# Rotary embedding: the exchange of rows inside SBUF by matrix product, or by sixteen-kilobyte transfers with the sign in the angle table

## What is computed

```python
def _partial_rope(t, cos, sin):
    tr = t[..., :ROT_DIM].astype(jnp.float32)            # ROT_DIM = 16
    t1, t2 = tr[..., :ROT_DIM // 2], tr[..., ROT_DIM // 2:]
    rot = jnp.concatenate([t1 * cos - t2 * sin, t2 * cos + t1 * sin], axis=-1)
    return jnp.concatenate([rot.astype(t.dtype), t[..., ROT_DIM:]], axis=-1)

q_a = _partial_rope(_rmsnorm_2(q_a.reshape(b, s, ATTN_HEADS, HEAD_DIM), g_qn_attn[l]), cos, sin)
k_a = _partial_rope(_rmsnorm_2(k_a.reshape(b, s, ATTN_HEADS, HEAD_DIM), g_kn_attn[l]), cos, sin)
```

## Time and profile before

| | us |
|---|---|
| median of 3 runs | 2988.92 (2987.07 to 2989.79) |
| span of the profiled execution | 2986.5 |
| PE busy with matrix products in it | 2817.0 (94%) |
| VectorE (DVE) busy | 1155.4 (39%) |
| ScalarE (ACT) busy | 556.1 (19%) |
| GpSimd (POOL) busy | 621.8 (21%) |

### The profile page before, as it was taken

How to read it: one execution, slowest core, us unless ns; L and a number is a source line. 1 busy time by engine, 2 the same in 40 slices (tenths; PEclk the granted TensorE clock), 3 DMA queues, 4 the chain that set the end, 5 groups by cost and what they waited for, 6 DMA issues and landing times.

```text
span 2986.5 us, 42182 instructions
## 1 busy us (share of the span) xinstructions
PE 2817.0 (94%) x18274; PEld 2423.2 (81%) x18274; DVE 1155.4 (39%) x2204; ACT 556.1 (19%) x856; POOL 621.8 (21%) x584
## 2 busy tenths in 40 slices
PE   8999999999999999999999999999999999866766
PEld 6888988889888899899988888889988888533433
DVE  3865235452433334745214344435355312210111
ACT  2101222124211101010033116210012330100000
POOL 0001411122121075068601210038800000000000
PEclk9999999999999999999999999999999999988878
DMA  9764543344443556764544444365433328899998
GB/s 406 297 263 163 175 150 134 121 141 171 140 141 127 196 199 229 272 219 166 183 147 143 139 153 143 130 224 170 165 135 130 105 91 351 381 432 430 430 430 371
DMA packets 74155, 641.62 MB, mean 215 GB/s; under 512 B 8304, under 2 KB 9584, under 8 KB 17648
## 3 DMA queue, kind: packets, MB, share of 16 engines
q1 hardware_dynamic: 71376, 631.55, 56.5%
q10 hardware_dynamic: 2592, 7.33, 0.6%
HBM read 637.80 MB, written 1.05 MB: 214 GB/s over the span
## 4 chain that ended last, share of the span: by engine, by line
PE 86%; DMA 12%; DVE 1%; issue 0%; ACT 0%; POOL 0%; SPq 0%; DVEq 0%; POOLq 0%; ACTq 0%
PE ps L1364 27%; PE ps L1340 20%; PE ps L1386 13%; DMA work<-in_w_moe 11%; PE ps L1561 7%; PE ps L1397 3%; PE ps L1591 2%; PE ps L1374 2%; PE ps L1145 2%; PE ps L1450 1%; PE ps L1167 1%; PE ps L1568 1%; PE ps L1272 1%; PE ps L1536 0%; PE ps L1539 0%; DMA ring<-in_w 0%
## 5 line engine op out<-in xcount | busy, mean ns | idle before, releaser
L2760 POOL TENSOR_TENSOR ring<-ring 128x512 f32<-128x512 f32 (+1 forms) x294 | 374.2, 1301 | 783.0 <-DMA ring<-in_w 315.7
L1364 PE MATMUL ps<-ring 128*128 128x256 f32 x2368 | 517.4, 380 | 0.6 <-ACT ring L1784 0.6
L1364 PEld LDWEIGHTS ps<-ring 128*128 128x128 f32 x2368 | 447.3, 190 | 63.2 <-issue 2.4
L2029 DVE TENSOR_TENSOR work<-work,ps 128x128 f32<-128x128 f32 (+3 forms) x534 | 185.6, 386 | 714.6 <-PE ps L1340 349.2
L1340 PE MATMUL ps<-work,ring 128*128 128x128 f32 x3312 | 385.8, 275 | 0.3 <-POOL work L2760 0.3
L1386 PE MATMUL ps<-work,ring 128*128 128x256 f32 x1760 | 385.5, 380 | 0.0
L1340 PEld LDWEIGHTS ps<-work,ring 128*128 128x128 f32 x3312 | 377.6, 192 | 0.5 <-POOL work L2760 0.5
L1386 PEld LDWEIGHTS ps<-work,ring 128*128 128x128 f32 x1760 | 332.5, 190 | 46.2 <-issue 2.1
L1364 PE MATMUL ps<-h,ring 128*128 128x256 f32 x1408 | 310.7, 382 | 6.5 <-ACT h L1784 2.9
L1364 PEld LDWEIGHTS ps<-h,ring 128*128 128x128 f32 x1408 | 265.8, 191 | 47.0 <-issue 5.7
L2029 DVE TENSOR_TENSOR work<-work 128x128 f32<-128x128 f32 (+4 forms) x566 | 261.6, 511 | 52.1 <-ACT eb L1812 24.9
(11 more groups left out here) (315 smaller groups left out, 2655.6 us busy)
## 6 DMA issues: line engine op xcount, KB each, us to landing
ring<-in_w SPq DMA_DIRECT2D x210, 1024.0 KB, 4.9
work<-in_w_moe SPq DMA_DIRECT2D x22, 4096.0 KB, 33.5
ring<-in_w_moe SPq DMA_DIRECT2D x22, 4096.0 KB, 33.4
ring<-in_w_in SPq DMA_DIRECT2D x80, 1024.0 KB, 4.9
work<-in_w_ada SPq DMA_DIRECT2D x40, 1024.0 KB, 6.1
ring<-in_w_ada SPq DMA_DIRECT2D x32, 1024.0 KB, 5.1
ring<-in_w SPq DMA_DIRECT2D x28, 768.0 KB, 4.2
ring<-in_w_out SPq DMA_DIRECT2D x16, 1024.0 KB, 5.1
```

The source lines that it names most:

```text
L1364: last = nc.tensor.matmul(ps[:, b, c * L:c * L + L], w[:, k * L + c * P:k * L + c * P + P], hs[cols][:, k, :], start=(k == 0), stop=(k == ...
L2029: return nc.vector.tensor_tensor(o, i0, i1, op)
L2760: return nc.gpsimd.tensor_tensor(o, i0, i1, ALU.subtract)
```

## The change

The product with `rot`, the matrix itself, its load and the semaphore `nq_rot` go. In the stage `rotate` ACT's queue now waits for `nq_done` (and, from the third on, for the DVE to be through with the rotation two before), and then issues four transfers inside SBUF, each of 8 partitions by 512 numbers (16 KB), which write the exchanged halves of the tile into `tmp2`. The DVE waits for all four, multiplies `tmp2` in place by the table of sines, and does the rest as before. `tmp2` is set to zero once, ahead of the DVE's first `nsum`, so that the rows that no transfer writes stay zero. The sign moves into the table: the frequencies of the first half are negated, which negates its sines and leaves the cosines.

```diff
@@ PE
-                    elif kind == "rotate":
-                        i = stage[1]
-                        pe.wait_ge(nq_done, i + 1)
-                        if i >= 2:
-                            pe.wait_ge(nq_roped, i - 1)
-                        nc.tensor.matmul(ps[:, 6 + i % 2, :], rot, normed(i), start=True, stop=True).then_inc(nq_rot, 1)
@@ ACT
-                        for dst, name in ((amask, "amask"), (blk64, "blk64"), (rot, "rot"), (rw[:], "rw"),
+                        for dst, name in ((amask, "amask"), (blk64, "blk64"), (rw[:], "rw"),
                                           (counting, "tri")):
...
+                    elif kind == "rotate":
+                        i = stage[1]
+                        act.wait_ge(nq_done, i + 1)
+                        if i >= 2:
+                            act.wait_ge(nq_roped, i - 1)
+                        for b in (0, 8, 64, 72):
+                            act.dma_start(tmp2[b:b + 8, i % 2], normed(i)[b ^ 8:(b ^ 8) + 8]).then_inc(nq_swapped[i % 2], 16)
@@ DVE
                     elif kind == "nsum":
                         i = stage[1]
+                        if i == 0:
+                            own(nc.vector.memset(tmp2, 0.0))
                         dve.wait_ge(nq_sum, i + 1)
...
-                        dve.wait_ge(nq_rot, i + 1)
+                        dve.wait_ge(nq_swapped[i % 2], 64 * (i // 2 + 1))
                         t2 = tmp2[:, i % 2, :, :]
-                        tt(t2, ps[:, 6 + i % 2, :].rearrange("p (c n) -> p c n", c=2),
-                           sinn[:].unsqueeze(1).to_broadcast([P, 2, L]), mul)
+                        tt(t2, t2, sinn[:].unsqueeze(1).to_broadcast([P, 2, L]), mul)
                         own(tt(normed(i), normed(i), cosn[:].unsqueeze(1).to_broadcast([P, 2, L]), mul))
                         tt(normed(i), normed(i), t2, add).then_inc(nq_roped, 1)
@@ layout
-    for b in (0, 8, 64, 72):
-        inv[b:b + 8, 0] = f
+    for b in (0, 64):
+        inv[b:b + 8, 0] = -f
+        inv[b + 8:b + 16, 0] = f
```

More of the change, by code:

```diff
@@ L601, in build @@
         blk64 = wsbs[:, 6 * L:6 * L + P]
-        rot = wsbs[:, 6 * L + P:6 * L + 2 * P]
         counting = st[:, 2:4, :].rearrange("p a b -> p (a b)")[:, 0:P + CAP]
@@ L711, in build @@
         nq_done = sem("nq_done")
-        nq_rot = sem("nq_rot")
+        nq_swapped = [sem(f"nq_swapped{i}") for i in range(2)]
         nq_roped = sem("nq_roped")
@@ L1601, in first @@
                         if i == 0:
-                            pe.wait_ge(late_in, 80)
+                            pe.wait_ge(late_in, 64)
                         pe.wait_ge(nq_sq, i + 1)
@@ L2526, in first @@
                         if u == 0:
-                            dve.wait_ge(late_in, 80)
+                            dve.wait_ge(late_in, 64)
                             tt(rw[:], rw[:], v("g_ffn", 0, KD).unsqueeze(2).to_broadcast([P, KD, 36]), mul).then_inc(rw_done, 1)
@@ L2836, in constants @@
     c["blk64"] = (s // 64 == t // 64).astype(f)
[L2837 to L2842, removed]
     c["tri"] = np.concatenate([(s <= t).astype(f), np.broadcast_to(np.arange(1, CAP + 1, dtype=f), (P, CAP))], 1)
```

## The result

| | us |
|---|---|
| before, median (5 runs) | 2988.92 (2987.07 to 2992.26) |
| changed, median (5 runs) | 3000.93 (2999.58 to 3004.99) |
| ratio, 95% interval | 1.0042 [1.0031, 1.0053] |
| span of the profiled execution, before and changed | 2986.5, 2999.1 |

The change makes the kernel slower by 0.42%, 12 us, and the profiled spans differ by 12.6 us. The page of the changed kernel shows almost the same busy times; nothing became more work.

The account below looks back on a forecast made before the run. PE was taken to bound the rotation stage by a hair, the DVE's loop being equally long. Delay to the sixth sum 8.85 plus clock 1.4 gave +10.2 us on 2988.9, so 2999 us; range 2992.5 to 3007.

Parts of the forecast that it names:

- The mechanism: Rotation stage: the exchange lies on the DVE's closed loop, which grows to 11.35 us against PE's step of 7.77.
- Which sums stall: PE's sums of squares for tiles 2 to 5 each wait for a late rotation, idling about 3.6 us per step.
- The landing L: Time from the fourth transfer's issue to its landing in SBUF: 2.4 us taken, bounds 1.6 and 4.9, counted four times.
- the way out: After rotation 3, slow rotations 4 and 5 delay the DVE's mean of tile 6: 2L - 4.5, +0.3 us at L = 2.4.
- Issues before the fourth: Three transfer issues on ACT's queue ahead of the fourth in each rotation: 1.4 us taken, bounds 0.1 to 1.5.
- Rival C: Transfer issues on ACT's queue nearly free, 0.1 us and not 0.45; +4.5 us, 2993 us; chance 0.13.
- Rival B: Transfers queue among a slab's packets, landing in 3.2 to 4.9 us; most likely about +18 us, 3007; chance 0.14.
- The clock, +1.4 us: PE's clock falls to 1.2 GHz through idling; uncovered after the last of four stalls, +1.4 us, bounds 0 and 2.8.
- 8.85: Delay in us up to the sixth sum of squares (tile 5), 4L - 0.75 at L = 2.4, removed products included.
- Part 4: The rest: DVE reading tmp2 from SBUF, clearing tmp2, one constant fewer, sign in the table: 0 us (clearing 1.4 without cover).

Follow-up runs that it names:

- square-first experiment: Changed kernel with the next square's stage ahead of the rotation in the list, so ACT squares tile i + 2 before waiting for rotation i's root: 3003.9 us, ratio 1.0057.

## Why the prediction was right, step by step

Forecast 2999.0, measured 3000.93; a loss of 10.2 us was forecast, 12.0 came (12.8 in the stage).

Some steps rest on rows of the changed kernel that were not shown yet. From the chain, the landings of rotations 0, 2 and 3 (that of rotation 1, at 2227.18, stands above):

```profile
2214.46 3.15 DMA work<-work
...
2238.98 2.51 DMA work<-work
...
2250.99 1.97 DMA work<-work
```

And from the timeline, the issues of rotation 5 and the square of tile 6 behind them:

```profile
2272.13 2.61 ACTq L1911 DMA_DIRECT2D work<-work  x4
2274.79 0.63 ACT L1900 ACTIVATE work<-ring 128x512 f32<-128x512 f32 x1 [2.99 <-issue]
```

- **The mechanism** (the DVE's loop was as long as PE's step, and the exchange lies on it): right, and shown by moving the rotation off the loop. The rotations start 11.47, 12.35 and 11.46 us apart, where 11.35 was forecast. The fixed part of 7.45 us is the same in the changed kernel (11.47 - 4.01 = 7.46).
- **Which sums stall** (four, tiles 2 to 5): right. But they don't stall alike: four waits of about 3.6 us were forecast, and 5.39, 1.12, 4.31 and 1.09 came, because the sum and slab behind a long wait ran at the low clock and filled most of the next one (see the clock below).
- **The landing L**, called the least certain: 2.4 was taken; the chain shows 3.15, 1.97, 2.51 and 1.97 for rotations 0 to 3, a mean of 2.4. The extrapolation from two loads was 0.1 too high for quiet engines (2.1 beside 1.97), and the 0.3 for loads in flight 0.1 too low (the four landings are 0 to 1.2 above 1.97, 0.4 in the mean). That the mean fell on 2.4 is in part luck: no rotation had it, and another execution of the same kernel has 3.17, 1.97, 2.81 and 1.97, a mean of 2.5. The Trainium skill, "DMA: Bandwidth & Descriptors", section "Anatomy of one DMA — SWDGE (gpsimd) path", gives a fixed cost of about 2.0 us plus the bytes for another kind of queue; the estimate of 2.04 from it agrees with the quiet landings here (1.97). The prediction said that its sum would then be 1.8 us smaller; by its own terms it is 4 x 0.36 = 1.4, since the 0.3 of the way out was not in the sum.
- **Issues before the fourth**: mis-sized. 1.4 us was taken from constants over 128 partitions; the transfers over 8 take the queue 0.63 us each and not 0.45 (the mean of the first three constants), and the first of all 1.26. The four issues of rotations 0 to 3 last 3.25, 2.62, 2.95 and 2.62 us together; less the last issue's 0.63, the fourth starts 2.6, 2.0, 2.3 and 2.0 us after the first. That is 8.9 us over the four rotations against 5.6, +3.3 us: the whole miss up to the sixth sum, which started 2260.23 - 2211.63 = 48.60 us after slab 3 and not 45.4.
- **Rival C**, nearly free issues: wrong in its sign. The issue came out longer and not shorter; whether the fewer rows made it so is open, since these transfers also differ from the constants in size and in where they read. By the Trainium skill, "DMA: Bandwidth & Descriptors", section "Issuing engines are not separate DMA queues", the time to initiate a transfer is usually small relative to the transfer itself. Here it was not small: one issue took 0.63 us beside a quiet landing of 1.97, and the three ahead of the fourth took 2.0 together.
- **Rival B**, transfers among a slab's packets: did not come as a case of its own, but is there in single loops, 2.5 and 3.2 us here and 4.7 with two transfers. I had it as one price for all four loops; which loops it hits depends on where the load falls, and changes with every edit.
- **The clock, +1.4 us**: the fall came (clock 0.84 over the stall) but its cost did not. It fell in every other step, and the last stall of 1.09 us found it high. With that term at 0, the sum is 8.85 + 3.3 = 12.1, and the way out gave 0.7 (forecast 0.3, swallowed): 12.8 us, the stage's loss. The forecast's total is as near as it is because two misses have opposite signs: 3.3 + 0.7 too little for issues and way out, 1.4 too much for the clock. The square-first experiment shows that the term was not wrong in kind: there the fall came last and cost 2.8.
- **The way out** had about the right size and another path. The forecast put it on the DVE, which would come late to tile 6's mean. What PE waited for was the square of tile 6 on ACT, and that stood behind the four issues of rotation 5 in ACT's own order. The issues began when the gain of tile 5 was done (2272.09) and ended at 2272.13 + 2.61 = 2274.74; the square began at 2274.79, and PE's sum waited 0.30 us for it. The forecast had counted the issues in the DVE's loop alone.
- **Part 4 and the later stages**: right. The memset took 0.91 us, and 12.64 us of idling still stood between it and the first mean; the sign costs nothing, and nothing was given back.

## What to carry to other kernels

Ask not how long an operation is but whether it lies on the loop that is next to the bound: 5.5 us less on PE became 12 us more because 1.2 us of latency became 4.0 on a loop with 0.1 us to spare. Here the transfers were worth their saving once issue and use stood in different rounds: moving the use by one round of the list turned 12.8 us more of stage into 5.5 less. A step that shortens a loop beside periodic loads can lose its gain to the next collision, so when gains are below 0.2% read stretches of the trace, not medians alone; and follow the gain to the end of the span, since a stretch that became shorter is not yet a shorter kernel.

## What the hardware did that I had not expected

- Issues of 16 KB transfers over 8 partitions, from SBUF to SBUF, take ACT's queue 0.63 us (24 of them, shortest 0.631, the first 1.256). The five constants, from HBM and over 128 partitions, took 0.35 to 0.56. Why is open.
- A 16 KB transfer landed in 1.97 us on quiet engines. Beside a slab's load it took 2.2 to 3.2 us in the changed kernel and up to 4.75 with two transfers, though the load came on another queue. With the loads held back it was 1.97 in each of five rotations.
- A DVE loop of 11.47 us made PE's clock alternate: a long stall, a slab at the low level (8.47 us), hence a short stall, a slab at the high level (7.07 us). The granted clock of 2225.2 to 2229.1 us was 0.50, the 1.2 GHz level, and of 2236.7 to 2241.5 it was 1.00:

```profile
2225.20:2229.10 3.90, 3.90 (x8) 2.43 (x9) 0.00 (x0) 0.18 (x1) 0.00 (x0) 0.50 0.09 17
2236.70:2241.50 4.80, 4.80 (x22) 3.83 (x22) 0.00 (x0) 0.15 (x1) 0.00 (x0) 1.00 0.51 208
```

The columns before the last are the clock and the share of the DMA engines: 0.09 where the transfers were alone, 0.51 beside a load.
